# One set of squares for two norms: the conv projections start from unscaled activations and get the token factors afterwards

## The reference, cut to what matters

```python
def rms_norm(x, g):
    y = x * rsqrt(mean(x * x, axis=-1) + 1e-6)
    return y * g

# end of the first network
x = x + squared_relu_mlp(rms_norm(x, norm_mlp[1]), w1, w2)
x = rms_norm(x, norm_final)                      # "norm 4" in the kernel
# start of the second
h = concatenate([meta_tokens, x])                # 16 + 256 tokens
z = rms_norm(h, g_mix) @ w_in                    # "norm 5" in the kernel
conv_val, conv_gate, rwkv_in, gate_logits = split(z)
u = conv_val * sigmoid(conv_gate)                # then a 31 tap convolution, and so on
...
h = h + (gate_a * y_a + gate_b * y_b) @ w_o      # the residual needs x of norm 4 itself
```

## Time and profile before

| | before |
|---|---|
| median of 3 runs | 1722.4 us (1721.68 to 1722.91) |
| the profiled execution's own time | 1721.23 us |
| its span in the trace | 1719.5 us |
| mean granted TensorE clock | 0.921 of full |
| PE busy / DVE busy / ACT busy | 1418.2 / 1081.0 / 561.8 us |

### The profile page before, as it was taken

How to read it: one execution, slowest core, us unless ns; L and a number is a source line. 1 busy time by engine, 2 the same in 40 slices (tenths; PEclk the granted TensorE clock), 3 DMA queues, 4 the chain that set the end, 5 groups by cost and what they waited for, 6 DMA issues and landing times.

```text
span 1719.5 us, 25059 instructions
## 1 busy us (share of the span) xinstructions
PE 1418.2 (82%) x9296; PEld 1075.0 (63%) x9296; DVE 1081.0 (63%) x2107; ACT 561.8 (33%) x1047; POOL 531.5 (31%) x620
## 2 busy tenths in 40 slices
PE   8999999986999997999988946867767649767675
PEld 7889999976999996878788832322222213222222
DVE  5556774486776445887765885676556457657444
ACT  5554653357564334423242113111111112111111
POOL 8100000010000000000000475666666666667573
PEclk9999999998999998999999977978888878999898
DMA  7344555543464543221243798999999999999996
GB/s 239 122 147 124 179 188 172 171 132 126 149 193 148 189 154 98 95 79 52 75 148 122 278 395 300 376 352 364 366 362 364 359 380 356 380 373 387 348 387 260
DMA packets 206242, 407.91 MB, mean 237 GB/s; under 512 B 10626, under 2 KB 136876, under 8 KB 206140
## 3 DMA queue, kind: packets, MB, share of 16 engines
q0 software_dynamic: 74096, 269.52, 40.9%
q1 hardware_dynamic: 131884, 136.54, 24.9%
q10 hardware_dynamic: 160, 0.53, 0.1%
HBM read 405.49 MB, written 1.05 MB: 236 GB/s over the span
## 4 chain that ended last, share of the span: by engine, by line
PE 50%; issue 17%; POOL 13%; DVE 9%; another core or an unknown queue 6%; ACT 3%; DMA 2%; POOLq 0%; DVEq 0%; SPq 0%; ACTq 0%
PE banks L2039 11%; PE banks L2041 11%; PE banks L2040 11%; POOL arena L869 5%; POOL wring L869 4%; PE banks L2217 4%; PE banks L2458 3%; POOL h_raw L869 2%; PE banks L2314 1%; PE banks L2208 1%; POOL xT L869 1%; POOL sq L869 1%; PE banks L2024 1%; DVE arena L1894 1%
## 5 line engine op out<-in xcount | busy, mean ns | idle before, releaser
L1337 DVE TENSOR_TENSOR w_a_low<-wring,w_a_high 128x1024 fp32r<-128x1024 f32 x184 | 225.2, 1226 | 130.3 <-ACT w_a_high L910 128.3
L869 POOL DMA_INDIRECT arena<-in_expert_u_dram,eidx x99 | 93.2, 942 | 674.6 <-DVEq L1874 610.6
L910 ACT ACTIVATE w_a_high<-wring 128x1024 fp32r<-128x1024 f32 x184 | 193.3, 1053 | 147.1 <-PE banks L2041 145.3
L2493 PE MATMUL banks<-arena 128*128 128x512 f32 x340 | 171.7, 652 | 72.2 <-issue 53.6
L1280 ACT ACTIVATE arena<-ident,arena 128x128 f32<-128x128 f32 x238 | 84.2, 395 | 442.6 <-remote 232.3
L2039 PE MATMUL banks<-h_high,w_a_high 128*128 128x256 f32 x768 | 219.3, 286 | 7.9 <-DVE h_low L1345 7.3
L2040 PE MATMUL banks<-h_low,w_a_high 128*128 128x256 f32 x768 | 216.6, 282 | 0.0
L2041 PE MATMUL banks<-h_high,w_a_low 128*128 128x256 f32 x768 | 216.5, 282 | 0.0
L2493 PE MATMUL banks<-wring,arena 128*128 128x512 f32 x308 | 152.9, 642 | 48.9 <-issue 37.0
L2493 PEld LDWEIGHTS banks<-arena 128*128 128x128 f32 x340 | 67.7, 207 | 174.9 <-issue 154.9
L2039 PEld LDWEIGHTS banks<-h_high,w_a_high 128*128 128x128 f32 x768 | 145.6, 190 | 9.7 <-issue 7.6
(11 more groups left out here) (395 smaller groups left out, 2886.6 us busy)
## 6 DMA issues: line engine op xcount, KB each, us to landing
wring<-in_mlp_w_dram SPq DMA_DIRECT2D x64, 1024.0 KB, 5.4
wring<-in_w_in_dram SPq DMA_DIRECT2D x19, 1024.0 KB, 5.2
wring<-in_sb_w_qkv_dram SPq DMA_DIRECT2D x12, 1024.0 KB, 5.1
wring<-in_rg_w_in_dram SPq DMA_DIRECT2D x8, 1024.0 KB, 5.9
wring<-in_w_q_dram SPq DMA_DIRECT2D x8, 1024.0 KB, 5.2
wring<-in_sb_w_o_dram SPq DMA_DIRECT2D x4, 1024.0 KB, 6.2
wring<-in_rg_w_o_dram SPq DMA_DIRECT2D x4, 1024.0 KB, 5.2
wring<-in_w_o_dram SPq DMA_DIRECT2D x4, 1024.0 KB, 7.7
```

Of the source, the lines that this page charges most:

```text
L869: g.indirect_dma_start(out=grow(j), out_offset=None, in_=(expert_u, expert_v)[which][0], in_offset=bass.IndirectOffsetOnAxis(ap=eidx[:, tt ...
L910: a.activation(unit(n, 0), raw_unit(n), ACT.Copy).then_inc(w_high, 1)
L1337: v.tensor_tensor(unit(n, 1), raw_unit(n), unit(n, 0).bitcast(F32), ALU.subtract).then_inc(w_split, 1)
L2493: last = mm(y_banks[tt][half][:, :], diag[:, n % DIAGS, :], grow(j)[:, 512 * half:512 * (half + 1)], start=False, stop=True, skip_group_ch ...
```

## The change

Norm 5's mean is taken over `x4 = xT * rs4 * norm_final`. Since rs4 is one factor per token, mean(x4²) = rs4² · mean(xT² · norm_final²), so both means come from the same squares of the unnormed `xT`: one with `mean_d`, one with a matrix `mean_g` whose rows are scaled by `norm_final²`. The conv products don't need the token factor either: `val` and `cg` are formed from `xT * (norm_final * g_mix)` and multiplied by the combined factor when DVE reads the banks.

- In the second MLP's down loop ACT and DVE now make, as tiles of `xT` become final, `h_high`, `h_low` and the squares (`last_input`), and once the learned tokens' part, `g_both`, `g_square` and `mean_g`.
- `val0` stands ahead of `ms4`, the group of norm 4's mean, and `ms5` (now 8 matmuls of 16 columns with `mean_d` and 8 of 256 with `mean_g`) behind it; then the other seven groups.
- DVE makes both reciprocals, ACT two roots one behind the other; DVE writes `hT` straight from `xT`, `g_both` and `rs`, then reads all eight banks with the factor; ACT's sigmoid works on SBUF behind it.
- DVE's three fills with constants and the write of norm 4's result to `xT` now stand behind the last `cg` group, ahead of `U`.
- The conv weights' parts lie in the ring `w_a`, like those ahead of them; `w_c` is gone.

```diff
-    plan.add("ms4")
-    plan.add("ms5")
     for m in range(RT):
         plan.add(f"val{m}")
+        if m == 0:
+            plan.add("ms4")
+            plan.add("ms5")
...
-            w = w_a if n < UNIT["w_conv"] else w_c if n < UNIT["rwkv_out"] else w_d
+            w = w_a if n < UNIT["rwkv_out"] else w_d
...
+            def last_input(kt):          # ACT
+                act.wait_ge(x_ready, KT * 4 + kt + 1)
+                a.activation(h_hl[0][:, kt, real], xT[:, kt, real], ACT.Copy,
+                             scale=g_both[:, kt:kt + 1]).then_inc(h_high, 1)
+                a.activation(sq[:, kt, real], xT[:, kt, real], ACT.Square).then_inc(sq_ready, 1)
...
+                split_high(18)
+                for kt in range(4):
+                    last_input(kt)
+                split_high(MLP_UNITS - hidden - UNITS - 18)
+                for kt in range(4, 6):
+                    last_input(kt)
+                split_high(3)
+                for kt in range(6, 8):
+                    last_input(kt)
+                split_high(2)
...
-            norm(4, after=UNITS)
-            norm(5, whole=2)
-
+            act.wait_ge(mean_ready, 5)
+            a.activation(rs[:, 0:TOK], rs[:, 0:TOK], ACT.Sqrt).then_inc(rs_ready, 1)
+            a.activation(rtmp[:, 0:SEQ], rtmp[:, 0:SEQ], ACT.Sqrt).then_inc(rs_ready, 1)
+            split_high(3)
             for m in range(RT):
-                pb = wait_group(act, f"val{m}")
-                split_high()
-                a.activation(val[:, m, :], pb[:, 0:TOK], ACT.Copy).then_inc(free(f"val{m}"), 1)
-            for m in range(RT):
-                pb = wait_group(act, f"cg{m}")
-                a.activation(cg[:, m, :], pb[:, 0:TOK], ACT.Sigmoid).then_inc(free(f"cg{m}"), 1)
+                wait_out(act, f"cg{m}")
+                a.activation(cg[:, m, :], cg[:, m, :], ACT.Sigmoid).then_inc(cg_ready, 1)
...
+            def last_input(first, last_):          # DVE
+                for kt in range(first, last_):
+                    dve.wait_ge(x_ready, KT * 4 + kt + 1)
+                    dve.wait_ge(h_high, KT * H_AT[5] + kt + 1)
+                    v.scalar_tensor_tensor(h_hl[1][:, kt, real], xT[:, kt, real], g_both[:, kt:kt + 1],
+                                           h_hl[0][:, kt, real].bitcast(F32), ALU.mult, ALU.subtract).then_inc(h_ready, 1)
...
-            split_low(UNITS)
-            norm(4, 4, xT)
...
-            norm(5, 13)
+            split_low(3)
+            pb = wait_group(dve, "ms4")
+            link(v.tensor_scalar(rtmp[:, 0:SEQ], pb[:, 0:SEQ], EPS, None, ALU.add))
+            dve.sem_inc(free("ms4"), 1)
+            link(v.reciprocal(rtmp[:, 0:SEQ], rtmp[:, 0:SEQ]))
+            pb = wait_group(dve, "ms5")
+            mark(v.tensor_copy(rs[:, 0:META], pb[:, 0:META]))
+            mark(v.tensor_tensor(rs[:, real], pb[:, real], rtmp[:, 0:SEQ], ALU.mult))
+            settle()
+            dve.sem_inc(free("ms5"), 1)
+            link(v.tensor_scalar(rs[:, 0:TOK], rs[:, 0:TOK], EPS, None, ALU.add))
+            link(v.reciprocal(rs[:, 0:TOK], rs[:, 0:TOK]))
+            link(v.tensor_tensor(rs[:, real], rs[:, real], rtmp[:, 0:SEQ], ALU.mult))
+            dve.sem_inc(mean_ready, 2)
...
+            for kt in range(KT):
+                v.scalar_tensor_tensor(hT[:, kt, real], xT[:, kt, real], g_both[:, kt:kt + 1], rs[:, real],
+                                       ALU.mult, ALU.mult).then_inc(h_whole, 1)
...
-            split_low(RT)
+            for name, dst in (("val", val), ("cg", cg)):
+                for m in range(RT):
+                    if name == "val" and m:
+                        split_low()
+                    pb = wait_group(dve, f"{name}{m}")
+                    v.tensor_tensor(dst[:, m, :], pb[:, 0:TOK], rs[:, 0:TOK], ALU.mult).then_inc(free(f"{name}{m}"), 1)
+            mark(v.memset(zf[:, :, 0:PADC], 0.0))
+            mark(v.memset(U[:, :, 0:CK - 1], 0.0))
+            mark(v.memset(aa[:, :, 0:LEAD], 0.0))
+            dve.wait_ge(rs_ready, RS_AT[5])
+            dve.wait_ge(h_whole, KT * (WHOLE_AT[5] + 1))
+            for kt in range(KT):
+                mark(v.scalar_tensor_tensor(xT[:, kt, real], xT[:, kt, real], pc(4, kt), rtmp[:, 0:SEQ],
+                                            ALU.mult, ALU.mult))
             for m in range(RT):
                 wait_out(dve, f"val{m}", f"cg{m}")
+                dve.wait_ge(cg_ready, m + 1)
                 mark(v.tensor_tensor(U[:, m, CK - 1:], val[:, m, :], cg[:, m, :], ALU.mult))
...
             mlp(1)
+            pe.wait_ge(meta_split, 1)
+            project(["val0"], "w_conv", h_all, ready=h_wait(5))
             norm(4)
-            norm(5)
-            project([f"{n}{m}" for n in ("val", "cg") for m in range(RT)], "w_conv", h_all, ready=h_wait(5))
+            pe.wait_ge(meta_high, 2)
+            pe.wait_ge(mean_g_ready, KT)
+            pb = open_bank("ms5")
+            for kt in range(KT):
+                mm(pb[:, 0:META], mean_d[:], sq[:, kt, 0:META], start=kt == 0, stop=kt == KT - 1)
+            for kt in range(KT):
+                last = mm(pb[:, real], mean_g[:, kt, :], sq[:, kt, real], start=kt == 0, stop=kt == KT - 1)
+            last.then_inc(group_done, 1)
+            project([f"val{m}" for m in range(1, RT)] + [f"cg{m}" for m in range(RT)], "w_conv", h_all, first=1)
```

More of the change, by code:

```diff
@@ L926, in mlp @@
                     split_high()
-                split_high(MLP_UNITS - hidden - UNITS)
+                if layer == 0:
+                    split_high(MLP_UNITS - hidden - UNITS)
+                    return
+                act.wait_ge(meta_ready, 1)
+                a.activation(h_hl[0][:, :, 0:META], meta_g[:], ACT.Copy).then_inc(meta_high, 1)
+                a.activation(sq[:, :, 0:META], xT[:, :, 0:META], ACT.Square).then_inc(meta_high, 1)
+                split_high(18)
[13 more added lines that the diff above has]
+                a.activation(sq[:, kt, real], xT[:, kt, real], ACT.Square).then_inc(sq_ready, 1)
             def norm(j, whole=0, units=False, after=0):
```

44 lines of the change are left out of this document (33 added, 11 removed).

## The result

The changed kernel took 1701.24 us (median of 4 runs, 1699.58 to 1701.31) against 1722.04 for the kernel before (4 runs): a ratio of 0.9889 [0.9872, 0.9906], or 20.8 us less. Forecast were 1709.0 us and a gain of 13.4. The direction was right; the gain was 7.4 us larger, and the time lies outside the range, under its lower end of 1705.5.

The account below looks back on a forecast made before the run. PE waiting for norms between the down projection and `zr` was taken as the bound. PE gains 15.5 us, DVE 10.1 plus 3.29 of absorbed waits; 1722.4 - 13.4 gives 1709.0 us, range 1705.5 to 1713.0.

Parts of the forecast that it names:

- What bounds the stage: Down projection to `zr`, 48.46 us: about half is PE waiting for norms; without these waits PE gains 15.5 us.
- The 16 column matmuls: Eight matmuls in `ms5` on PE, estimated from transposes at 1.8 us, with bounds of 0 and 3.46.
- The end of the stage on DVE: DVE's work behind the last conv group takes 6.73 us to the first tap, which starts 10.1 us earlier.
- The backlog: DVE's 3.29 us of waits for ACT's copies fall away before the shift at 705.44, making the gain 13.4 us.
- DVE is the later one: At the shift of line 1562 DVE comes 2.2 us after PE, so the gain there is 13.4 us.
- PE's 15.5: Rival, chance 0.15: DVE catches up between 705 and 746, so the gain is PE's 15.5 us: 1706.9 us.
- The lead is not usable: Rival, chance 0.20: DVE keeps its waits (1712.3 us), or PE idles longer before 746 and its clock drops (1711.4).
- What is added in the down loop: Added ACT and DVE work in the down loop fits into their waits and was costed at nothing.
- behind 746.04 nothing is changed, in instructions or in order: The program after PE's wait at 746.04 is unchanged, so the 13.4 us is carried to the end.

Follow-up runs that it names:

- the runs with 32 and 64 increments: Kernel before plus 32 or 64 unused semaphore increments on PE between norm 4's and norm 5's mean: 1646.33 us (ratio 0.9970) and 1645.29 us (0.9953).
- the cut loads: Kernel before with seven eighths of two gate weight loads (fourth and fifth) left out: 1647.88 us against 1651.15, ratio 0.9977.

## Why the prediction was right, and where it failed

- **What bounds the stage** was right. PE's stage went from 48.46 to 32.92 us, against 32.9 forecast; `val0` started at once, and the last `h_low` was ready at 644.48, 0.4 us ahead of the last tile of `val0` (644.92), which is the cover that was forecast, and nothing waited for the factors: `hT` was written by 661.58, against 661.4.
- **The 16 column matmuls** took 650.46 - 648.75 = 1.71 us from start to start, 1.85 with the drain, against 1.8 by the transposes. The floor of about 25 ns that the Trainium skill states (TensorE: Matmul & The Clock Gate, "Wait — 56ns, not 53.3ns?"), taken as the cost, gave an estimate of 0.4. The row shows 0.107 us for each of the 16, so the floor isn't what sets their pace; the measurement decides.
- **The end of the stage on DVE** took 681.43 - 675.18 = 6.25 us, against 6.73: the eight multiplications stand 3.04 apart in place of 3.35, and 0.2 is in small steps.
- **The backlog** was right in mechanism and size: DVE lost all its waits for ACT's copies, and the shift came at 691.85 against 692.04. Measured from the down projection's end, which was 0.57 later than before in this execution (its start was, too), the stage up to DVE's line 1723 gained 14.2 us, against 13.4. That the absolute times agreed is luck of 0.57 us against 0.75: 0.48 came at the stage's end, and 0.27 from the first tap to the shift (10.42 against 10.69). I had chosen "DVE is the later one" over PE's 15.5, and the chain stays on DVE.
- **The lead is not usable**: no. PE, further ahead, does idle at two places before 732.38, 1.08 and 2.84 us, where it idled 2.68 before; it costs nothing, as DVE sets the time there.
- **What is added in the down loop** at nothing: right. From its first matmul to the instruction behind it, it takes 93.72 before (547.97 to 641.69) and 93.70 after (548.56 to 642.26).
- **The step that failed** is "behind 746.04 nothing is changed, in instructions or in order", from which the rest of the program was carried over at no gain. The order was unchanged, and the stretch still gained 5.6 us. PE's two gaps, 1.34 and 2.08 us, became one of 0.41, and the 3.6 us at a granted clock of 0.53 behind the second, 1.7 us of loss, went with them: 3.0 + 1.7 = 4.7 us, which is what the stretch up to the row of `head_mean` gained (109.74 to 105.00). That such gaps can be had or lost with no change in the work is shown by the runs with 32 and 64 increments; that a load takes part in the second, by the cut loads. That the change removed them by shifting PE's instructions rests on its 34 more of them: with 32 increments in the kernel before, the same stretch takes 104.93 us (746.25 to 851.18), and fetches and remaining gap stand at the same instructions. So most of the miss was a side effect of splitting norm 5's mean into two sets of matmuls, and no part of the idea.
- **The other 0.8 us of the 5.6** are clock. Behind PE's next two waits (4.5 and 6.1 us in both kernels) the granted clock over 10 us was 0.75 and 0.80 before (from 877.8 and 916.4), 0.83 and 0.84 after (from 859.4 and 897.5). The stretch from the row of `head_mean` to the first gather takes 103.9 to 105.5 us in the eleven other traces, whose code there is the same, and repeats within 0.1 in the changed kernel (104.13, 104.20). No run shows what decides it. The 0.9 in the gathers stay open too.

The gain was 7.4 us above the forecast: 0.8 up to line 1723, 5.6 behind it, 0.9 in the gathers, and 0.1 between medians and profiled executions. I had read the rows of the two gaps before the forecast and passed them over, because idle time "<-issue" in an untouched stretch seemed a property of the stretch. The range took in no case for it, though 3.4 us of such gaps stood in view. Had I priced it as a rival (both gaps go: 3.4 + 1.7 = 5.1, so 1703.9 us), the range would have reached under 1704, and still not to 1701.24.

## What to carry to other kernels

When a factor per row multiplies a product, form the product first and multiply where the result is read anyway; its price is read from the engine that reads (here 6.25 us of DVE behind the last group in place of 1.31), its worth from the wait it takes away (9.8 us). Before costing the rest of a program at zero, look through the bounding engine's rows for idle time that nothing releases: it can come or go with any edit that adds or removes instructions ahead of it, the measured change included, and two or three variants with a few idle instructions in a covered wait show how much of a difference is the edit and how much is the shift. Compare such variants by a distance inside the trace that repeats (0.13 us here) sooner than by the time of runs (several us).

## What the runs showed of the hardware

- PE stood still for 1.34 and 2.08 us with all inputs ready. 16 idle instructions put some 100 us earlier left that as it was, 32 took one gap away and the other down to 0.35, 64 removed both, 128 made four other gaps. Each of these gaps stood at a border between blocks of 256 instructions of PE, and ended 2.2 to 2.8 us behind the start of a 16 KB fetch.
- Semaphore increments on PE's queue started 0.15 us apart (64 in 9.6 us, 128 in 19.5): a cheap-looking instruction, dearer than a 128x256 matmul, which starts every 0.12 us in the down projection.
- The 16 records of the float32 matmuls of 16 columns, each with a load of a 128x128 matrix, took 0.107 us each.
- The same program took 1722, 1651, 1726 and 1651 us in four sets of runs, the last three on three chips. From the first gather to the end the kernel before takes 758.8 us in the first set, at a granted clock of 0.86 and 359 GB/s of DMA, and its variant with 64 increments 688.0 in the second (1645.5 - 957.5), at 0.97 and 396 GB/s, so nearly all of the difference is behind the first gather; the distance from the down projection to the first gather is the same to a few tenths. Why the gathers run slower in one set isn't shown.
